# Second attention of a two-block model: scores of the next head's shorter units ahead of this head's short transposes

## What is computed

```python
def mla_attention(q_nope, q_rope, k_nope, k_rope, v, q_chunk_blocks, k_chunk):
    L = k_nope.shape[1]
    scale = (MLA_NOPE + MLA_ROPE) ** -0.5
    def block(args):
        qn, qr, qc = args
        mask = k_chunk[None, :] <= qc[:, None]
        s = (jnp.einsum('bqhd,bkhd->bhqk', qn, k_nope)
             + jnp.einsum('bqhr,bkr->bhqk', qr, k_rope)).astype(jnp.float32) * scale
        p = jax.nn.softmax(jnp.where(mask, s, -jnp.inf), axis=-1)
        return jnp.einsum('bhqk,bkhd->bqhd', p.astype(v.dtype), v)
```

## Time and profile before

| | us |
|---|---|
| median of 3 runs | 2017.94 (2017.82 to 2018.52) |
| the profiled execution | 2019.1, its span 2017.3 |
| TensorE matmul busy | 2005.1 (99%) |
| TensorE weight loads busy | 1806.3 (90%) |
| VectorE, GpSimd, ScalarE busy | 1316.3, 1163.4, 851.3 |

### The profile page before, as it was taken

The page is one execution under the profiler, slowest core; times in us unless marked ns, Lnnn a source line. Parts: engine busy times, 40 slices in busy tenths (PEclk is TensorE's granted clock), DMA queues, the critical chain, the costliest instruction groups (busy, mean ns, idle before and its releaser), DMA issues.

```text
span 2017.3 us, 37442 instructions
## 1 busy us (share of the span) xinstructions
PE 2005.1 (99%) x13376; PEld 1806.3 (90%) x13376; DVE 1316.3 (65%) x2202; ACT 851.3 (42%) x1502; POOL 1163.4 (58%) x1395
## 2 busy tenths in 40 slices
PE   9999999999999999999999999999999999999998
PEld 9999999999999988999999988777788888988987
DVE  7777857857646777757857678765512457857654
ACT  5554534432423577634433426344432234433433
POOL 6554456666757512156666768644455557666764
PEclk9999999999999999999999999999999999999999
DMA  5222123232323211022232323322222223232322
GB/s 191 84 74 78 61 89 97 83 108 84 106 94 116 84 43 43 28 84 94 84 126 84 116 89 109 106 74 84 84 93 96 84 84 98 80 125 84 126 84 84
DMA packets 51986, 183.06 MB, mean 91 GB/s; under 512 B 5648, under 2 KB 7824, under 8 KB 51856
## 3 DMA queue, kind: packets, MB, share of 16 engines
q1 hardware_dynamic: 50304, 178.87, 27.1%
q10 hardware_dynamic: 1552, 2.42, 0.4%
HBM read 179.17 MB, written 2.10 MB: 90 GB/s over the span
## 4 chain that ended last, share of the span: by engine, by line
PE 94%; DVE 3%; DMA 1%; issue 1%; ACT 1%; POOL 1%; SPq 0%; DVEq 0%; ACTq 0%
PE ps L814 25%; PE ps L815 24%; PE ps L816 24%; PE ps L939 3%; PE ps L940 3%; PE ps L941 3%; PE ps L1196 2%; PE ps L1218 1%; PE ps L1100 1%; PE ps L1211 1%; PE ps L1131 1%; POOL w_lo L768 1%; PE ps L887 1%; DMA h<-x_t 0%; DMA w_raw<-stream 0%
## 5 line engine op out<-in xcount | busy, mean ns | idle before, releaser
L748 POOL TENSOR_TENSOR w_lo<-w_raw,w_hi 128x256 fp32r<-128x256 f32 x1140 | 962.5, 879 | 736.1 <-ACT w_hi L2329 725.4
L814 PE MATMUL ps<-x_hi,w_hi 128*128 128x264 f32 (+2 forms) x2504 | 820.0, 327 | 0.1
L815 PE MATMUL ps<-x_lo,w_hi 128*128 128x264 f32 (+2 forms) x2504 | 813.6, 325 | 0.0
L816 PE MATMUL ps<-x_hi,w_lo 128*128 128x264 f32 (+2 forms) x2504 | 812.3, 324 | 0.0
L814 PEld LDWEIGHTS ps<-x_hi,w_hi 128*128 128x128 f32 x2504 | 471.3, 188 | 48.1 <-issue 5.4
L815 PEld LDWEIGHTS ps<-x_lo,w_hi 128*128 128x128 f32 x2504 | 470.9, 188 | 40.3 <-issue 0.2
L816 PEld LDWEIGHTS ps<-x_hi,w_lo 128*128 128x128 f32 x2504 | 471.4, 188 | 39.5
L2329 ACT ACTIVATE w_hi<-w_raw 128x1024 fp32r<-128x1024 f32 x267 | 278.0, 1049 | 69.7 <-PE ps L816 53.8
L814 PE MATMUL ps<-g_hi,w_hi 128*128 128x264 f32 (+3 forms) x648 | 207.5, 320 | 0.2 <-issue 0.2
L815 PE MATMUL ps<-g_lo,w_hi 128*128 128x264 f32 (+3 forms) x648 | 205.9, 318 | 0.0
L816 PE MATMUL ps<-g_hi,w_lo 128*128 128x264 f32 (+3 forms) x648 | 205.7, 317 | 0.0
(11 more groups left out here) (294 smaller groups left out, 3049.3 us busy)
## 6 DMA issues: line engine op xcount, KB each, us to landing
w_raw<-stream SPq DMA_DIRECT2D x334, 512.0 KB, 3.5
h<-x_t SPq DMA_DIRECT2D x4, 528.0 KB, 7.5
out_t<-h SPq DMA_DIRECT2D x6, 256.0 KB, 2.3
scratch<-rotary_tables ACTq DMA_DIRECT2D x4, 264.0 KB, 5.3
out_t<-h ACTq DMA_DIRECT2D x2, 256.0 KB, 2.5
par<-params ACTq DMA_DIRECT2D x1, 342.0 KB, 5.0
scratch<-positions ACTq DMA_DIRECT2D x1, 256.0 KB, 2.7
cst<-shape_constants ACTq DMA_DIRECT2D x1, 193.0 KB, 6.0
```

Of the source, the lines that this page charges most:

```text
L748: last = nc.gpsimd.tensor_tensor(w_lo[:, ring(j), cols], w_raw[:, j % 4, cols], w_hi[:, ring(j), cols].bitcast(F32), ALU.subtract)
L814: nc.tensor.matmul(out_ap, w_hi[:, s, c], xh[:, k, cols], start=first, stop=False)
L815: nc.tensor.matmul(out_ap, w_hi[:, s, c], xl[:, k, cols], start=False, stop=False)
L816: return nc.tensor.matmul(out_ap, w_lo[:, s, c], xh[:, k, cols], start=False, stop=last)
```

## The change

In head_b of TensorE the scores of units 2 to 4 of the next head and the transposes of units 2 to 4 of this head trade places. All waits, PSUM addresses and the other engines' programs stay.

```diff
--- before.py
+++ after.py
@@ -1251,11 +1251,11 @@
                     pe.wait_ge(o_taken_b, 5 * h)
                 if fills[0]:
                     fills[0]()
-                for idx in range(2, 5):
-                    transposes_b(h, idx)
                 if more:
                     for idx in range(2, 5):
                         scores_of_b(h + 1, idx)
+                for idx in range(2, 5):
+                    transposes_b(h, idx)
                 values_of_b(h, 0, 1).then_inc(pv_done_b, 2)
                 if fills[1]:
                     fills[1]()
```

## The result

| | before | after |
|---|---|---|
| median | 2017.94 (7 runs, 2017.64 to 2018.73) | 2025.14 (7 runs, 2023.17 to 2026.24) |
| profiled execution, its span | 2019.1, 2017.3 | 2024.47, 2022.7 |
| first load of the heads' scores to the end of the last values | 142.43 | 149.40 |

The changed kernel is slower: ratio 1.0034, 95% interval 1.0024 to 1.0043, 7.2 us by the medians. It lies in the forecast range (2022.0 to 2029.5), 1.1 us under the predicted 2026.2.

What follows compares the result with a forecast made beforehand. TensorE, busy 99% of the span, was taken as the bound. Gaps of 6.9 us plus 1.4 for the values' wait made 8.3 us, giving 2026.2 us; the range was 2022.0 to 2029.5.

Steps and rivals of the forecast that it cites:

- Step 1: Transposes no longer fill TensorE's wait for unit 0's exponential of the next head before the scores: 5.1 us added idle.
- step 3: Lost cover and ScalarE's loop combined, head by head: head 14's scores of units 2 to 4 plus transposes end 6.9 us later.
- Step 2: Later transposes delay take_rest_b and ScalarE's queue behind it up to the next head's first exponential: 9.24 us loop in head 2.
- (a): Cover before the scores is lost but ScalarE catches up within each head: +5.1 us, 2023.0, chance 0.20.
- Step 4: Values of units 2 and 3 (line 1218) wait 0.2 us for take_rest_b in eight heads: 1.4 us taken, bounds 0 and 3.2.
- The rule weighed there: If weight loads ran ahead across the semaphore, some ten stalls would be 0.1 us shorter each, the sum about 7.3.
- (b): Hardly any loss, as the first exponential comes earlier on ScalarE: +0 to +4 us, middle 2020.0, chance 0.10.
- (c): Faster: earlier scores in heads 1, 5, 9, 14 remove the 4.1 us of waits at line 1196: 2013.8, chance 0.04.
- (d): Gaps in heads 0 and 4 make TensorE's granted clock fall: 17 us more, 2043, chance 0.04.
- the lateness passes on to the end unabsorbed: Behind the attention TensorE stays busy with no transfer wait to absorb lateness, so all of the loss reaches the end.

Runs made afterwards that it cites:

- run with hi_part early: ScalarE's hi_part of heads 1 to 12 moved ahead of take_rest_b, against the changed kernel: median 2022.40 us, ratio 1.0023 to before, stretch 146.57.
- run of heads 1, 5, 9 and 14: Kernel before with next-head scores ahead of the transposes in those four heads only: median 2017.67 us, ratio 0.9999, stretch 142.59.
- new layout in the old order: Kernel before with 80 key columns of unit 0 moved from bank 4 to bank 2, unit 0's exponential awaiting both maxima: median 2020.08 us, ratio 1.0011.
- old order with hi_part early: Kernel before with ScalarE's hi_part moved ahead of take_rest_b in all its heads: median 2018.62 us, ratio 1.0004, stretch 143.35.
- heads 2, 6 and 10: Kernel before with next-head scores ahead of the transposes in those three heads only: median 2020.68 us, ratio 1.0015, stretch 144.95.

## Why the prediction was right, and where not

**Step 1 and step 3, the gaps.** S − S of head 0 in the table of the prediction and in the trace of after:

| head | predicted | measured |
|---|---|---|
| 2 | 19.22 | 19.33 |
| 4 | 37.72 | 37.66 |
| 7 | 66.18 | 66.12 |
| 11 | 102.97 | 102.86 |
| 14 | 127.93 | 127.93 |

All fourteen lie within 0.12 us. The gaps from arrival to S: head 0 1.00 (1.00 predicted), head 2 0.60 (0.59), head 4 1.49 (1.52), and no gap in heads 1, 5, 9 and 14, as forecast. Heads 3, 7 and 11 had 0.63 instead of 0.81: the loop through ScalarE was 9.10 and not 9.24, since T follows S after 0.84, not 1.04, and line 2658 could start at S + 1.84, not 2.00. The three gaps are 0.54 smaller together, and the pair S, T gave back 0.6, 0.04 in each of 15 heads. Neither had I foreseen; that the two nearly cancel is luck, and the 6.9 us of step 3 measured 6.97.

**Step 2, the carry-over**, which rival (a) denied. The traces have it in head 3. Counted from the start of the stretch, E ends at 36.96 before and at 38.76 after, 1.80 later, while TensorE's arrival moved by 1.38 (36.80 to 38.18). So of the gap of 0.63 there, 0.42 is carried over and 0.21 is the lag of step 1. Three such heads make 1.3, and 5.1 of step 1, 1.3 and the pair's 0.6 give the measured 7.0. The run with hi_part early shows the way it takes: 2.84 us of the 6.97 go with a shorter queue on ScalarE. That is more than the 1.3, as E then comes earlier also where it was late in the old order, in heads 3, 4, 7 and 11.

**Step 4, the wait of the values**, failed: 1.4 predicted, 0 measured. No row of line 1218 waits for line 2659 in after. The timeline of head 4 shows why: line 2659 is done at 760.99, S + 2.72, where I had reckoned S + 2.88, and the first pass of units 2 and 3 stands around 761.0. I had placed the values 0.03 too early and the copies 0.16 too late, both from taking S's and T's lengths of the old order over into the new one. Of the gap of 0.25 (rounded to 0.2 there) that leaves 0.06, less than the 0.07 that I had added for the signal. The wait is real, only just not reached: the new layout in the old order has it in head 0 (0.21), and the old order with hi_part early in four heads (0.16 or 0.17). This term, 1.4, is more than the 1.1 us by which the predicted 8.3 exceeds the measured 7.2; without it the prediction would have been 2024.8, against 2025.14 measured.

**The rule weighed there**, that TensorE pulls loads ahead of matmuls in flight (the Trainium skill, TensorE: Matmul & The Clock Gate, the table at its head), would have made each stall 0.1 shorter. The load in head 4 started 0.05 behind the end of E, after idling the whole 1.44; it was not pulled across the wait. Among blocks without a wait the trace agrees with the rule: with S first, T's first load starts at 759.11, while S's last matmul ends at 759.37 in the profile (758.27 + 1.10, a modelled end).

**The rivals.** (a), +5.1, lies inside the interval of the ratio (4.8 to 8.7 us), so the time alone doesn't rule it out; the stretch does, as above. (b), at most +4, and (c), faster, fall with the result, and (c) also with the run of heads 1, 5, 9 and 14. (d): the granted clock stayed at 1.00 through the stretch, with a gap of 1.44 us in it. The Trainium skill says (same page, Part 4) that transposes don't count as busy in the same way; no run here shows that, for or against. That the lateness passes on to the end unabsorbed was right. From the end of the stretch to the end of the program two traces with the same waits at line 939 (last section) need 1163.21 us before and 1163.07 after.

## What to carry to other kernels

An instruction that has nothing to wait for and stands in front of a wait is cover, and its price when moved is read from how far the awaited event lies behind the engine's arrival, head by head. Then follow what is queued behind the moved instruction's consumer on its own in-order engine, once around to the same place; if that loop is longer than the first engine's own, the loss is more than the cover. And take the loop with the new order's lengths and count each block as often as the engine passes it, which is where two of my sums went wrong: step 4 and the expectation for heads 2, 6 and 10.

## What the runs showed of the chip

The spread of the times comes from places far from the change. The stretch starts at anything from 709.96 to 713.36 us in the eleven traces, with the same program up to there. The waits of TensorE ahead of line 939, in the first feed-forward, from 0 to 708 us, in the first trace of before (start 711.66):

```profile
PEld ps L939 <- issue: 1.5, 2, 1.2
```

and in the old order with hi_part early (start 713.36):

```profile
PEld ps L939 <- issue: 2.5, 2, 1.4
PE ps L939 <- ACT sq L2354: 2.2, 2, 1.2
```

The two traces of after, which start at 710.23 and 710.07, have only two gaps of at most 0.3 at line 939 and none for line 2354. So an execution has none, one or two gaps of about 1.2 to 1.4 us there. Even without one the start lies between 709.96 and 710.90.

The part behind the stretch differs too, and again at line 939, in later stages. The second trace of before, from 860 us on, with 1164.0 us behind the stretch:

```profile
PEld ps L939 <- issue: 1.5, 2, 0.9
PE ps L939 <- DVE h L1610: 1.1, 2, 0.7
```

Two of the eleven traces have two such gaps and need 1163.8 and 1164.0 us there, four have one and need 1163.1 to 1163.2, five have none and need 1162.4 or 1162.5. A difference of a tenth or two of a per cent between two single executions can be this alone. What causes it was not tried. Comparing the changed stretch by itself, which repeats to 0.01 us, tells apart what the time of the whole program hardly can.
